# Block two's layer norms: column six closed in the last product, partial sums among its matmuls, five square buffers

## The chip, the cores and the metric

The kernel runs on one core of a Trainium2 chip. The metric is the device time of one execution in microseconds. TensorE, VectorE, ScalarE and GpSimd work side by side from instruction queues of their own and wait for each other by counters; SyncE issues most of the loads.

## The reference

Two transformer blocks stand one behind the other on x (1 x 512 tokens x 1024), float32, two layers each. The change touches only the second. Each of its layers is

```python
def _layer_norm(x, g, b):
    xf = x.astype(jnp.float32)
    mu = xf.mean(-1, keepdims=True)
    var = jnp.square(xf - mu).mean(-1, keepdims=True)
    return ((xf - mu) * lax.rsqrt(var + LN_EPS)).astype(x.dtype) * g + b

    h = x * (1.0 + sc1) + sh1
    y = _token_mixer(h, ...)
    x = _layer_norm(ALPHA * x + g1 * y, ln1_g[l], ln1_b[l])
    h = x * (1.0 + sc2) + sh2
    y = _conv_ffn(h, ...)
    x = _layer_norm(ALPHA * x + g2 * y, ln2_g[l], ln2_b[l])
```

so there are four of these norms in an execution: one (layer 0, "mix"), two (layer 0, "ffn"), three (layer 1, "mix") and four (layer 1, "ffn", whose result is the output).

## The kernel before, in words

**Layout.** X lies in SBUF transposed: eight chunks ("columns", 0 to 7) of 128 channels x 512 tokens. A mean over the channels is a sum over the eight chunks and over the partitions; the latter is a matmul with a 128 x 128 matrix of ones.

**Products.** Weights come in panels of 1 MB (raw, three slots, SyncE). Each is split for exactness into a high part (ScalarE, `split_hi`, line 754, two slots) and a low part (VectorE, `split_lo`, line 760, in the raw panel's place). The operand is split likewise (Hhi/Hlo, Mhi/Mlo, Uhi/Ulo). A chunk of a product is three matmuls, lines 782, 783 and 789. A panel gives two output columns, each summed over nk chunks (8; 6 in the last part of the FFN's down product). Where `k_outer` is set, the first panel behind a norm runs over the chunks outside, so that it can begin with the first normed chunk.

**Order.** One Python list of items (`Schedule`) is walked by every engine, and each takes from it what is its own, in that order. `product` puts the high and low split of the next panel behind a quarter of a panel's steps. All waits are on counters of the instruction that made the datum.

**The end of a branch.** `out_stages` and the last part of `ffn_stages` have four panels (p = 0 to 3), two columns each. `evict` of a column on VectorE is, from line 2081: a residual scaling (2092 or 2095; in the FFN it was done with the first part), for columns 4 to 7 a shift by -2/D times the sum of the first four columns (line 2106), and the addition of the gated product from PSUM (line 2111). That half mean mh is made behind half of panel 2: GpSimd adds columns 0 to 3 into sx (line 1698), TensorE sums it (line 2275). Columns 0 to 3 get their shift afterwards (line 2117).

**Squares and sums.** Each shifted column is squared on ScalarE (line 1837; two buffers) and added on GpSimd into qa (line 1708), in the order 0, 1, 4, 2, 3, 5, 6; xa (line 1714) adds columns 4, 5 and 6, which stand in for all because the shift made the first four's part known. Column 7 and its square are not added.

**`lnend`.** After the four panels TensorE sums, in this order, xa and qa (lines 2283, 2284), X seven (2286, same bank as xa) and square seven (2289, same bank as qa). ScalarE makes the squared mean (1842) and the mean msb (1843); VectorE the variance (2125) and X zero minus mean (2129); ScalarE the root (1845, behind a load of its table); VectorE the reciprocal (2131). GpSimd subtracts the mean from columns 1 to 7 (1720).

**`lnx`, `lnlo`.** Per column VectorE multiplies by the reciprocal (2138), ScalarE makes the high half and the full value of the next operand (1851, 1854) or the output (1857), VectorE the low half (2142). The next item is the first product, and a quarter into it the split of the second panel.

In the "mix" norm of layer 0, GpSimd issues two loads of tables (lines 1684, 1685) between its last xa and its subtractions.

Of the kernel before, what the change touches and what calls it, by code (L numbers as in the profile page):

```python
# [16 lines left out]
P = 128  # L17
# [13 lines left out]
FFN_PARTS = ((0, 8), (8, 8), (16, 6))  # L31
A_HEADS = 8
# [70 lines left out]
class Schedule:  # L103
# [19 lines left out]
    def split_ahead(self, n):  # L123
        while self.splits < min(n + 1, len(self.planned)):
            self.add("split", self.splits, self.planned[self.splits][1])
            self.splits += 1
# [15 lines left out]
    def product(self, n, nk, width, cols, rhs, k_outer=False, midway=None):  # L142

        self.begin(n)
        for _, job in cols:
            self.wide.take(job)
        self.last_use[n] = cols[-1][1]
        if k_outer:
            steps = [(k, cc, job) for k in range(nk) for cc, job in cols]
        else:  # L150
            steps = [(k, cc, job) for cc, job in cols for k in range(nk)]
        quarter, half = len(steps) // 4, len(steps) // 2
        self.add("mm", n, width, steps[:quarter], nk, rhs)
        self.split_ahead(n + 1)
        self.add("mm", n, width, steps[quarter:half], nk, rhs)
        if midway:
            midway()
        self.add("mm", n, width, steps[half:], nk, rhs)
# [287 lines left out]
def out_stages(s, n, l, column, between=lambda: None, halfway=None):  # L446

    for p in range(4):
        s.product(n, 8, 256, [(j, ("out", l, 2 * p + j)) for j in range(2)], ("M", l), k_outer=(p == 0),
                  midway=halfway if p == 2 else None)  # L450
        n += 1
        between()
        for c in (2 * p, 2 * p + 1):
            s.add("evout", l, c)
            column(c)
# [3 lines left out]
def ffn_stages(s, n, l, column, between=lambda: None, root=None, halfway=None):  # L459

    for part, (u0, nu) in enumerate(FFN_PARTS):
# [22 lines left out]
        last = part == len(FFN_PARTS) - 1  # L484
        for p in range(4):
            s.product(n, nu, 256, [(j, ("down", l, part, 2 * p + j)) for j in range(2)], ("U", l, part),
                      k_outer=(p == 0), midway=halfway if last and p == 2 else None)
            n += 1
            between()
            for c in (2 * p, 2 * p + 1):  # L490
                s.add("evdown", l, part, c)
                if last and column:
                    column(c)
    return n


def schedule_two():
# [6 lines left out]
    for l in range(DEPTH):  # L504
# [111 lines left out]
        n = out_stages(s, n, l, lambda c: ln_column(s, l, "mix", c), halfway=lambda: ln_half(s, l, "mix"))  # L616
        if l + 1 < DEPTH:
            s.add("tables", l + 1)
        layer_norm_stages(s, l, "mix", (l, "ffn"))
        n = ffn_stages(s, n, l, lambda c: ln_column(s, l, "ffn", c), halfway=lambda: ln_half(s, l, "ffn"))  # L620
        layer_norm_stages(s, l, "ffn", (l + 1, "mix") if l + 1 < DEPTH else None)
    return s

# [7 lines left out]
SQUARED = (0, 1, 4, 2, 3, 5, 6)  # L631


def ln_column(s, l, w, c):
# [3 lines left out]
    for i in {4: (0, 1, 4), 5: (2, 3, 5), 6: (6,), 7: (7,)}.get(c, ()):  # L638
        if i > 0:
            s.temp("sq", 2, ("sq", l, w, i))  # L640
        s.add("lnsq", l, w, i)


def layer_norm_stages(s, l, w, after):

    s.small.take(("mn", l, w))
    s.small.take(("ss", l, w))
    s.temp("rs", 2, ("rs", l, w))
    s.add("lnend", l, w)
    for k in range(DC):  # L650
# [5 lines left out]
    if after:  # L656
        s.add("lnlo", *after, DC - 1)

# [273 lines left out]
def block_one(nc, io, known, banks=None):  # L932
    from contextlib import ExitStack
    s = schedule_one()
    with ExitStack() as ctx:
# [174 lines left out]
        def _(act):  # L1110
# [8 lines left out]
            for kind, *a in s.items:  # L1119
                if kind == "sines":  # L1120
                    build_tables(nc, None, act, steps, "tab1", None, None, [t[:] for t in tab_tmp], cos[:], sin[:], None)
                elif kind == "split":
# [110 lines left out]
        def _(dve):  # L1233
            dve.wait_ge(gain_landed, 16)
            for kind, *a in s.items:
# [7 lines left out]
                elif kind == "split":  # L1243
# [310 lines left out]
def block_two(nc, io, known):  # L1554
    from contextlib import ExitStack
    s = schedule_two()
    with ExitStack() as ctx:
        def sem(name):
# [12 lines left out]
        coef = mem.put("coef", [P, 3, 4, 8])  # L1571
        ulow = mem.at
# [36 lines left out]
        msb = mem.again(ulo_at + 8 * SEQ * 4, area).put("msb", [P, SEQ])  # L1609
# [12 lines left out]
                    fa=fa, silu=silu, fw=fw, fv=fv)  # L1622
# [35 lines left out]
        def at_col(j):  # L1658
            return (0, 512, 896, 1152)[j]

# [16 lines left out]
        def _(pool):  # L1677
            for kind, *a in s.items:
# [21 lines left out]
                elif kind == "lnsq" and a[2] not in (0, 7):  # L1700
                    l, w, c = a
                    i = SQUARED.index(c)
                    pool.wait_ge(*after("sq", l, w, c))
                    if i == 1:
                        pool.wait_ge(*after("sq", l, w, 0))
                    else:
                        pool.wait_ge(*after("qa", l, w, SQUARED[i - 1]))
                    ng.tensor_tensor(qa[:], qa[:], k.sq[slot("sq", ("sq", l, w, c))][:], ALU.add)\  # L1708
                        .then_inc(*mark("pool", ("qa", l, w, c), ("free", ("sq", l, w, c))))
                    if c >= 5:  # L1710

                        if c == 6:
                            pool.wait_ge(*after("xa", l, w, 5))
                        ng.tensor_tensor(xa[:], X[:, 4] if c == 5 else xa[:], X[:, c], ALU.add)\
                            .then_inc(*mark("pool", ("xa", l, w, c)))
# [35 lines left out]
        def _(act):  # L1751
# [6 lines left out]
            for kind, *a in s.items:  # L1758
                if kind == "split":
# [71 lines left out]
                elif kind == "lnsq":  # L1831
                    l, w, c = a
                    dst = qa[:] if c == 0 else buf(("sq", l, w, c))
                    if c > 0:
                        reuse(act, ("sq", l, w, c))
                    act.wait_ge(*after("xc", l, w, c))
                    act_e.activation(dst, X[:, c], ACT.Square).then_inc(*mark("act", ("sq", l, w, c)))
# [39 lines left out]
        def _(dve):  # L1877
# [19 lines left out]
            for kind, *a in s.items:  # L1897
                if kind == "split":
# [182 lines left out]
                elif kind == "evout" or kind == "evdown":  # L2081
# [7 lines left out]
                    if part == 0:  # L2089
                        ready = ("scaled", l, w, c)  # L2090
                        if l == 0 and w == "mix":
                            nv.tensor_scalar(X[:, c], X[:, c], ALPHA, None, ALU.mult).then_inc(*mark("dve", ready))
                        else:
                            by = (l, "mix") if w == "ffn" else (l - 1, "ffn")
                            nv.tensor_scalar(X[:, c], X[:, c], normed(*by, 2, c), normed(*by, 3, c), ALU.mult, ALU.add)\
                                .then_inc(*mark("dve", ready))
# [348 lines left out]
```

## Time and profile before

| | |
|---|---|
| median of 3 runs | 3611.62 us (3606.71 to 3614.3) |
| the profiled execution | 3609.19 us, span 3607.4 us |
| mean granted clock of TensorE | 0.973 |
| busy: TensorE, VectorE, ScalarE, GpSimd | 93%, 59%, 36%, 18% |
| block two's four norms, end of the product before | 2178.7, 2563.3, 3199.3, 3582.3 us |

Times in rows are in us from the start of the span. A timeline row is: start, length, engine, line, operation, written tile <- read tiles, shape, count of like ones in a row; in brackets the idle time of the engine before it and what ended it. A 512-wide float32 matmul with ones shows as two records (x2). Tiles of one name are told apart by their lines. PE is TensorE, DVE VectorE, ACT ScalarE, POOL GpSimd.

### The profile page before, as it was taken

To read this page: it belongs to the slowest core of one execution; us is meant where nothing else is said; L and a number is where in the kernel's file an instruction comes from. 1 tells how busy PE (TensorE), PEld (TensorE's weight loads), DVE (VectorE), ACT (ScalarE), POOL (GpSimd) and SP (SyncE) were. 2 spreads that over 40 slices of the span, in tenths; PEclk is the share of its full clock that TensorE was granted. 3 is DMA by queue.
4 is the path that set the end of the run, shared out by engine and by line. 5 is a ranking of instruction groups with operands and counts; after the bars stand their busy time and mean duration, and the time that the engine had idled before them with its cause. 6 is when DMAs were issued, how large, how long until landed. Compare 5 with 4: busy or idle time off the path is not lost. (4 is left out here: it accounts for less than half of the span.)

```text
span 3607.4 us, 38854 instructions
## 1 busy us (share of the span) xinstructions
PE 3369.9 (93%) x15280; PEld 2678.6 (74%) x15280; DVE 2142.4 (59%) x2729; ACT 1283.3 (36%) x1648; POOL 634.0 (18%) x507
## 2 busy tenths in 40 slices
PE   7899999999999999959988998999899979989997
PEld 5677788876677788847776886888677768868886
DVE  7853666448744765437986336554568864365545
ACT  4664322235653322223223324243432232243333
POOL 1122222121212311210001123010300002131003
PEclk9999999999999999979999999999999989999998
DMA  3122445321224453221211222222211112322221
GB/s 121 44 67 82 181 187 196 108 94 54 54 75 155 179 194 143 70 91 70 70 53 53 88 99 83 94 101 92 76 66 64 65 47 70 105 70 100 94 94 70
DMA packets 72181, 344.44 MB, mean 95 GB/s; under 512 B 25152, under 2 KB 26048, under 8 KB 35648
## 3 DMA queue, kind: packets, MB, share of 16 engines
q1 hardware_dynamic: 70560, 340.17, 27.0%
q8 instruction: 122, 2.00, 0.2%
q0 software_dynamic: 432, 1.28, 0.2%
q10 hardware_dynamic: 1008, 0.51, 0.0%
q14 instruction: 59, 0.48, 0.0%
HBM read 340.51 MB, written 2.10 MB: 95 GB/s over the span
## 5 line engine op out<-in xcount | busy, mean ns | idle before, releaser
L782 PE MATMUL bank_b<-Hhi_b,whi_b 128*128 128x512 f32 x2976 | 1228.3, 413 | 106.0 <-DVE wlo_b L760 52.2
L783 PE MATMUL bank_b<-Hhi_b,wlo_b 128*128 128x512 f32 x2976 | 1176.0, 395 | 0.0
L789 PE MATMUL bank_b<-Hlo_b,whi_b 128*128 128x512 f32 x2976 | 1165.3, 395 | 0.8 <-DVE Hlo_b L2142 0.8
L760 DVE TENSOR_TENSOR wlo_b<-raw_b,whi_b 128x2048 fp32r<-128x2048 f32 (+2 forms) x290 | 625.4, 2157 | 572.4 <-ACT whi_b L754 572.2
L782 PEld LDWEIGHTS bank_b<-Hhi_b,whi_b 128*128 128x128 f32 x2976 | 570.5, 192 | 257.8 <-issue 80.3
L783 PEld LDWEIGHTS bank_b<-Hhi_b,wlo_b 128*128 128x128 f32 x2976 | 570.1, 192 | 125.8 <-issue 14.3
L789 PEld LDWEIGHTS bank_b<-Hlo_b,whi_b 128*128 128x128 f32 x2976 | 567.6, 191 | 126.1 <-DVE Hlo_b L2142 3.0
L754 ACT ACTIVATE whi_b<-raw_b 128x2048 fp32r<-128x2048 f32 (+2 forms) x290 | 511.4, 1764 | 370.6 <-PE bank_b L789 370.5
L782 PE MATMUL bank_b<-Uhi_b,whi_b 128*128 128x512 f32 x1024 | 407.5, 398 | 0.0
L783 PE MATMUL bank_b<-Uhi_b,wlo_b 128*128 128x512 f32 x1024 | 401.4, 392 | 0.0
L789 PE MATMUL bank_b<-Ulo_b,whi_b 128*128 128x512 f32 x1024 | 387.8, 392 | 0.0
L871 POOL TENSOR_TENSOR Ulo_b<-fv_b,Uhi_b 128x512 fp32r<-128x512 f32 x88 | 114.0, 1296 | 712.3 <-ACT Uhi_b L868 712.3
L782 PEld LDWEIGHTS bank_b<-Uhi_b,whi_b 128*128 128x128 f32 x1024 | 192.2, 188 | 47.2 <-issue 4.6
L783 PEld LDWEIGHTS bank_b<-Uhi_b,wlo_b 128*128 128x128 f32 x1024 | 192.2, 188 | 43.7 <-issue 1.9
L789 PEld LDWEIGHTS bank_b<-Ulo_b,whi_b 128*128 128x128 f32 x1024 | 192.1, 188 | 43.6
L1948 DVE SCALAR_TENSOR_TENSOR acc_b<-Up_b,vec_b,acc_b 128x512 f32<-128x512 f32 x240 | 192.2, 801 | 4.7
L1083 POOL TENSOR_TENSOR silu_b<-silu_b,RX_b 128x512 f32<-128x512 f32 x44 | 100.6, 2289 | 405.5 <-DVE silu_b L1447 405.5
L868 ACT ACTIVATE Uhi_b<-fv_b 128x512 fp32r<-128x512 f32 x88 | 55.6, 633 | 288.0 <-DVE fv_b L1454 168.8
L1099 POOL TENSOR_SCALAR sc_b<-sc_b,rec_b 128x256 f32<-128x256 f32 (+1 forms) x128 | 87.1, 693 | 371.6 <-DVE rec_b L1392 371.6
L857 POOL TENSOR_TENSOR ym_b<-ym_b,mt_b 128x512 f32<-128x512 f32 x48 | 67.7, 1414 | 383.6 <-DVE mt_b L849 383.6
L1417 DVE CUSTOM_DVE_ANT_0 ada_b<-ada_b,cond_b,bada_b 128x1024 f32<-128x1024 f32 x96 | 134.6, 1439 | 0.0
L871 POOL TENSOR_TENSOR Ulo_b<-ON_b,Uhi_b 128x512 fp32r<-128x512 f32 x16 | 22.3, 1396 | 602.8 <-ACT Uhi_b L868 602.8
(244 smaller groups left out, 3493.8 us busy)
## 6 DMA issues: line engine op xcount, KB each, us to landing
raw_b<-in_w SPq DMA_DIRECT2D x234, 1024.0 KB, 4.9
ada_b<-in_wada SPq DMA_DIRECT2D x48, 1024.0 KB, 7.0
raw_b<-in_w SPq DMA_DIRECT2D x40, 512.0 KB, 3.6
raw_b<-in_w SPq DMA_DIRECT2D x16, 768.0 KB, 4.3
rel_b<-in_rel SPq DMA_DIRECT2D x128, 24.0 KB, 2.4
X_keep<-in_x SPq DMA_DIRECT2D x4, 512.0 KB, 8.6
out<-X_keep SPq DMA_DIRECT2D x8, 256.0 KB, 2.1
cond_b<-in_c SPq DMA_DIRECT2D x2, 512.0 KB, 4.4
```

The lines of the kernel that those rows point to most:

```text
L754: self.nc.scalar.activation(self.whi[n % HI_SLOTS][:, 0:words], self.raw[n % RAW_SLOTS][:, 0:words], ACT.Copy).then_inc(*self.steps.mark(" ...
L760: self.nc.vector.tensor_tensor(self.wlo[n % RAW_SLOTS][:, 0:words], self.raw[n % RAW_SLOTS][:, 0:words], self.whi[n % HI_SLOTS][:, 0:words ...
L782: self.nc.tensor.matmul(out, whi[:, k, cols], xhi, start=(k == 0), stop=False)
L783: self.nc.tensor.matmul(out, wlo[:, k, cols], xhi, start=False, stop=False)
L789: mm = self.nc.tensor.matmul(out, whi[:, k, cols], xlo, start=False, stop=(k == nk - 1))
L857: nc.gpsimd.tensor_tensor(y, y, k.mt[k.slot("mt", mt)][:], ALU.add)\
L868: nc.scalar.activation(hi, src, ACT.Copy).then_inc(*steps.mark("act", ("hi",) + name))
L871: nc.gpsimd.tensor_tensor(lo, src, hi.bitcast(F32), ALU.subtract)\
L1083: nc.gpsimd.tensor_tensor(g, g, RX[:], ALU.mult).then_inc(*mark("pool", ("silu", l, c)))
L1099: nc.gpsimd.tensor_scalar(p, p, rec[:, i % 2, j:j + 1], 1.0, ALU.mult, ALU.mult)\
L1417: nc.vector.tensor_tensor_reduce(w, w, cond[:], 1.0, bada[:, l, j:j + 1], ALU.mult, ALU.add, keep.mod[:, l, j:j + 1]).then_inc(*mark("dve" ...
L1948: nv.scalar_tensor_tensor(out=acc[:, c], in0=src, scalar=w, in1=acc[:, c], op0=ALU.mult, op1=ALU.add).then_inc(*mark("dve", ("cv", l, c, t ...
```

## The change

1. `product` takes a table of hooks (step to action) and a switch for the split ahead. In the last panel of `out_stages` and `ffn_stages` there is no split at the quarter.
2. For p = 1 to 3 the eviction of the first column of a panel stands in the list at the half of the panel, not behind it.
3. Column six: its residual scaling and shift, and those of column seven, are items of their own behind column five (`lnshift`). Its eviction stands behind half of the last panel.
4. `lngather` on TensorE, before that eviction: sum of xa (now columns 4 and 5 alone) and sum of qa (without six). `lnsix`, half a column and a step later: sums of X six and of square six. Behind the product only the sums of X seven and square seven are left.
5. On GpSimd xa is one addition, before the last of qa's five.
6. Five buffers for squares (`lsq`): the old two and three more in the area of the mean.
7. ScalarE does a root of one element behind square six (`idle_root`), so that its table is loaded there; behind it stand both splits of the first panel after the norm.
8. The high split of the second panel (`round`) stands behind `lnend`, the low one (`rest`) behind the last `lnlo`.
9. GpSimd subtracts the mean from columns 1 to 6, VectorE from column 7, just before its multiplication.
10. The table loads of layer 1 stand behind the norm.

```diff
-    def product(self, n, nk, width, cols, rhs, k_outer=False, midway=None):
+    def product(self, n, nk, width, cols, rhs, k_outer=False, hooks=None, ahead=True):
...
+        hooks = dict(hooks or {})
+        if ahead:
+            hooks[len(steps) // 4] = lambda: self.split_ahead(n + 1)
+        at = 0
+        for stop in sorted(hooks):
+            self.add("mm", n, width, steps[at:stop], nk, rhs)
+            hooks[stop]()
+            at = stop
+        self.add("mm", n, width, steps[at:], nk, rhs)
...
+def closing_hooks(s, l, w, nk, p, middle):
+
+    if p == 0:
+        return {}
+    if p < 3:
+        return {nk: middle}
+
+    def gathered():
+        s.small.take(("mn", l, w))
+        s.small.take(("ss", l, w))
+        s.add("lngather", l, w)
+        middle()
+
+    return {nk: gathered, nk + nk // 2 + 1: lambda: s.add("lnsix", l, w)}
...
     for i in {4: (0, 1, 4), 5: (2, 3, 5), 6: (6,), 7: (7,)}.get(c, ()):
         if i > 0:
-            s.temp("sq", 2, ("sq", l, w, i))
+            s.temp("lsq", 5, ("lsq", l, w, i))
         s.add("lnsq", l, w, i)
+    if c == 5:
+        s.add("lnshift", l, w, 6)
+        s.add("lnshift", l, w, 7)
+    if c == 6:
+        s.split_ahead(n)
...
     s.add("lnend", l, w)
+    if after:
+        s.round_next()
     for k in range(DC):
...
     if after:
         s.add("lnlo", *after, DC - 1)
+        s.rest_next()
...
+                    if c == 5:
+                        ng.tensor_tensor(xa[:], X[:, 4], X[:, 5], ALU.add).then_inc(*mark("pool", ("xa", l, w)))
+                    ng.tensor_tensor(qa[:], qa[:], buf(("lsq", l, w, c)), ALU.add)\
+                        .then_inc(*mark("pool", ("qa", l, w, c), ("free", ("lsq", l, w, c))))
...
-                    for c in range(1, DC):
+                    for c in range(1, DC - 1):
                         ng.tensor_tensor(X[:, c], X[:, c], msb[:], ALU.subtract).then_inc(*mark("pool", ("xm", l, w, c)))
...
+                    if c == 6:
+
+                        i = 2 * l + (w == "ffn")
+                        act_e.activation(idle_root[:, i:i + 1], keep.eps[EPS2][:, 0:1], ACT.Sqrt)\
+                            .then_inc(*mark("act", ("root table", l, w)))
...
+                elif kind == "lnshift":
+                    l, w, c = a
+                    ready = ("xp", l, 1, c)
+                    if w == "mix":
+                        ready = ("scaled", l, w, c)
+                        residual(l, w, c)
+                    shift_column(dve, ready, l, w, c)
...
+                    if c == DC - 1:
+                        nv.tensor_tensor(X[:, c], X[:, c], msb[:], ALU.subtract).then_inc(*mark("dve", ("xm", l, w, c)))
...
-                elif kind == "lnend":
+                elif kind == "lngather":
                     l, w = a
                     mn, ss = ("mn", l, w), ("ss", l, w)
                     reuse(pe, mn)
                     reuse(pe, ss)
-                    pe.wait_ge(*after("xa", l, w, 6))
+                    pe.wait_ge(*after("xa", l, w))
                     nt.matmul(k.out_of(mn)[:], keep.ones[:], xa[:], start=True, stop=False, skip_group_check=True)
+                    pe.wait_ge(*after("qa", l, w, 5))
                     nt.matmul(k.out_of(ss)[:], keep.ones[:], qa[:], start=True, stop=False, skip_group_check=True)
+                elif kind == "lnsix":
+                    l, w = a
+                    pe.wait_ge(*after("xc", l, w, 6))
+                    nt.matmul(k.out_of(("mn", l, w))[:], keep.ones[:], X[:, 6], start=False, stop=False,
+                              skip_group_check=True)
+                    pe.wait_ge(*after("lsq", l, w, 6))
+                    nt.matmul(k.out_of(("ss", l, w))[:], keep.ones[:], buf(("lsq", l, w, 6)), start=False, stop=False,
+                              skip_group_check=True).then_inc(*mark("pe", ("free", ("lsq", l, w, 6))))
```

## Rows read from the trace of the kernel before

**Rows 1.** The page's first part: busy us, share of the span.

```profile
PE 3369.9 (93%) x15280; PEld 2678.6 (74%) x15280; DVE 2142.4 (59%) x2729; ACT 1283.3 (36%) x1648; POOL 634.0 (18%) x507
```

**Rows 2.** Timeline of TensorE around the four norms, behind its waits.

```profile
2182.53 1.69 PE L2283 MATMUL bank_b<-xa_b,ones_keep 128*128 128x512 f32 x2 [3.84 <-POOL xa_b L1714]
...
2212.32 0.47 PE L782 MATMUL bank_b<-Hhi_b,whi_b 128*128 128x512 f32 x1 [2.66 <-issue]
...
2568.58 2.03 PE L2283 MATMUL bank_b<-xa_b,ones_keep 128*128 128x512 f32 x2 [5.33 <-POOL xa_b L1714]
...
3232.98 0.47 PE L782 MATMUL bank_b<-Hhi_b,whi_b 128*128 128x512 f32 x1 [1.13 <-ACT fa_b L1865]
...
3584.57 1.10 PE L2283 MATMUL bank_b<-xa_b,ones_keep 128*128 128x512 f32 x2 [2.25 <-POOL xa_b L1714]
```

**Rows 3.** Timeline of TensorE, the half mean's sum inside a product.

```profile
2160.93 1.02 PE L2275 MATMUL bank_b<-sx_b,ones_keep 128*128 128x512 f32 x2
2161.39 0.80 PE L782 MATMUL bank_b<-Mhi_b,whi_b 128*128 128x512 f32 x1
```

**Rows 4.** Timeline of GpSimd in norms one and four.

```profile
2169.80 4.18 POOL L1708 TENSOR_TENSOR qa_b<-qa_b,sq_b 128x512 f32<-128x512 f32 x3 [1.51 <-ACT sq_b L1837]
2173.93 3.37 POOL L1714 TENSOR_TENSOR xa_b<-X_keep 128x512 f32<-128x512 f32 x1
...
2188.24 9.96 POOL L1720 TENSOR_TENSOR X_keep<-X_keep,msb_b 128x512 f32<-128x512 f32 x7 [4.79 <-ACT msb_b L1843]
...
3573.64 7.07 POOL L1708 TENSOR_TENSOR qa_b<-qa_b,sq_b 128x512 f32<-128x512 f32 x5 [6.29 <-ACT sq_b L1837]
...
3583.17 1.26 POOL L1714 TENSOR_TENSOR xa_b<-xa_b,X_keep 128x512 f32<-128x512 f32 x1
```

**Rows 5.** Timeline of VectorE in norms one, two and four.

```profile
2164.66 0.42 DVE L2092 TENSOR_SCALAR X_keep<-X_keep 128x512 f32<-128x512 f32 x1
...
2167.64 0.75 DVE L2111 SCALAR_TENSOR_TENSOR X_keep<-bank_b,mod_keep,X_keep 128x512 f32<-128x512 f32 x1 [1.84 <-PE bank_b L789]
...
2188.03 0.69 DVE L2125 SCALAR_TENSOR_TENSOR rs_b<-bank_b,m_b 128x512 f32<-128x512 f32 x1 [7.09 <-PE bank_b L2289]
...
2190.22 3.35 DVE L2131 RECIPROCAL rs_b<-rs_b 128x512 f32<-128x512 f32 x1 [0.18 <-ACT rs_b L1845]
...
2196.97 1.77 DVE L2142 TENSOR_TENSOR Hlo_b<-hf_b,Hhi_b 128x512 fp32r<-128x512 f32 x1
...
2208.12 0.69 DVE L2142 TENSOR_TENSOR Hlo_b<-hf_b,Hhi_b 128x512 fp32r<-128x512 f32 x1 [0.72 <-ACT hf_b L1854]
2209.93 2.29 DVE L760 TENSOR_TENSOR wlo_b<-raw_b,whi_b 128x2048 fp32r<-128x2048 f32 x1 [1.11 <-ACT whi_b L754]
...
2576.27 3.35 DVE L2131 RECIPROCAL rs_b<-rs_b 128x512 f32<-128x512 f32 x1 [0.18 <-ACT rs_b L1845]
...
3574.28 0.75 DVE L2111 SCALAR_TENSOR_TENSOR X_keep<-bank_b,mod_keep,X_keep 128x512 f32<-128x512 f32 x1 [0.85 <-PE bank_b L789]
...
3578.36 0.75 DVE L2111 SCALAR_TENSOR_TENSOR X_keep<-bank_b,mod_keep,X_keep 128x512 f32<-128x512 f32 x1 [1.53 <-PE bank_b L789]
...
3592.05 3.35 DVE L2131 RECIPROCAL rs_b<-rs_b 128x512 f32<-128x512 f32 x1 [0.18 <-ACT rs_b L1845]
```

**Rows 6.** Timeline of ScalarE, norm one: the load before the root.

```profile
2188.18 1.28 ACT L1845 ACT_TABLE_LOAD   x1
```

**Rows 7.** Windows of TensorE: stretch, busy (count), granted clock, DMA share, GB/s.

```profile
2212.00:2218.00 6.00, 5.68 (x18) 0.72 0.29 122
3214.00:3224.00 10.00, 6.58 (x15) 0.50 0.00 0
3232.00:3240.00 8.00, 7.02 (x31) 1.00 0.38 131
```

**Rows 8.** Timeline of ScalarE in block one: roots, then a square.

```profile
80.89 0.63 ACT L1179 ACTIVATE qa_b<-qa_b 128x512 f32<-128x512 f32 x1
81.43 0.58 ACT L1164 ACTIVATE sq_b<-bank_b 128x512 f32<-128x512 f32 x1
```

More of the change, by code:

```diff
@@ L484, in ffn_stages, with evict @@
         last = part == len(FFN_PARTS) - 1
+        split = last and halfway
         for p in range(4):
[L486 to L490, printed above, removed]
+            def evict(c):
                 s.add("evdown", l, part, c)
@@ L493, in ffn_stages, with middle @@
                     column(c)
+            def middle():
+                if p == 2:
+                    halfway()
+                evict(2 * p)
+            s.product(n, nu, 256, [(j, ("down", l, part, 2 * p + j)) for j in range(2)], ("U", l, part),
+                      k_outer=(p == 0), hooks=closing_hooks(s, l, "ffn", nu, p, middle) if split else None,
+                      ahead=not split or p < 3)
+            n += 1
+            between()
+            if not split or p == 0:
+                evict(2 * p)
+            evict(2 * p + 1)
     return n
@@ L1571, in block_two @@
         coef = mem.put("coef", [P, 3, 4, 8])
+        idle_root = mem.put("idle_root", [P, 4])
         ulow = mem.at
@@ L1608, in block_two @@
         qa, xa, sx, m2 = (lnb.put(n, [P, SEQ]) for n in ("qa", "xa", "sx", "m2"))
-        msb = mem.again(ulo_at + 8 * SEQ * 4, area).put("msb", [P, SEQ])
+        lnb = mem.again(ulo_at + 8 * SEQ * 4, area)
+        msb, *more_sq = (lnb.put(n, [P, SEQ]) for n in ("msb", "sq2", "sq3", "sq4"))
         mm_ = mem.again(past_tables, end)
@@ L1659, in at_col, with residual, shift_column @@
             return (0, 512, 896, 1152)[j]
+        def residual(l, w, c):
+            if l == 0 and w == "mix":
+                nv.tensor_scalar(X[:, c], X[:, c], ALPHA, None, ALU.mult).then_inc(*mark("dve", ("scaled", l, w, c)))
+            else:
+                by = (l, "mix") if w == "ffn" else (l - 1, "ffn")
+                nv.tensor_scalar(X[:, c], X[:, c], normed(*by, 2, c), normed(*by, 3, c), ALU.mult, ALU.add)\
+                    .then_inc(*mark("dve", ("scaled", l, w, c)))
+        def shift_column(dve, ready, l, w, c):
+            dve.wait_ge(*after(*ready))
+            dve.wait_ge(*after("mh", l, w))
+            names = [("free", ("mh", l, w))] if c == DC - 1 else []
+            nv.scalar_tensor_tensor(out=X[:, c], in0=k.out_of(("mh", l, w))[:], scalar=-2.0 / D, in1=X[:, c],
+                                    op0=ALU.mult, op1=ALU.add).then_inc(*mark("dve", ("xs", l, w, c), *names))
         block = ctx.enter_context(nc.Block())
@@ L2088, in _ @@
                     ready = ("xp", l, part - 1, c)
-                    if part == 0:
+                    if part == 0 and c < 6 or part == 0 and w == "ffn":
                         ready = ("scaled", l, w, c)
[L2091 to L2096, printed above, removed]
-                    name, names = ("xp", l, part, c), []
+                        residual(l, w, c)
+                    name = ("xp", l, part, c)
                     if last and c < 4:
```

94 lines of the change are left out of this document (46 added, 48 removed).

## The prediction

> **What bounds the kernel now.** I read the page's shares first, then the longest idle times of TensorE, then VectorE, ScalarE and GpSimd around the four norms of block two. The reader should see in [rows 1] that TensorE is busy for 93% of the span: only what lies in its idle time can be won, apart from its clock. Around a norm it is idle three times, and two of them have rows here [rows 2]. It ends the last product (2178.69, which is 2182.53 less 3.84 of waiting), waits for GpSimd's xa, does the four sums, waits for the first normed chunk, and waits 2.66 us more at the second panel (2212.32). The xa waits are 3.84, 5.33 and 2.25 us in norms one, two and four; norm three repeats norm one. After the sums VectorE and ScalarE are a chain: variance, root, reciprocal (3.35 us), eight chunks.
>
> **The sums inside the product.** A 512-wide sum put between product matmuls at the full clock is seen once per norm already, the half mean. Without it the next matmul would have started at 2160.93 and ended 0.40 later; it ended at 2161.39 + 0.80 [rows 3]. So one costs 0.86 us. Four of them now stand in or behind the sums' place: xa and qa in the middle, X six and its square later, 4 x 0.86 = 3.44 us longer product. X seven and its square stay behind it.
>
> **The wait that moves in with them.** The gathering stands after half of the last product, and TensorE takes its queue in order, so all remaining matmuls stand behind it. Is xa ready there? It is queued on GpSimd behind the adds of one, four, two and three; five of them take 7.07 us in a row, 1.41 each [rows 4]. *FFN norms:* the adds begin at 3573.64, xa at 3573.64 + 4 x 1.41 = 3579.28, takes 1.26 as the add of 3583.17 did, and the hand-over to TensorE costs 0.14 (3584.43 to 3584.57 [rows 2, 4]): 3580.7. Column six is done 4.08 us after column five: their evictions start at 3574.28 and 3578.36 [rows 5], so TensorE is there at 3578.2. It waits 2.5 us; qa then is ready 0.4 us later than its turn: 2.9 us. Norm two has the same code and shapes up to there, and I take the same. *Mix norms:* the product runs from about 2167.5 (column five's eviction starts at 2167.64, 0.11 behind it) to 2178.69, so its half ends at 2173.1 [rows 2, 5]. The three adds began at 2169.80; after two of them xa would start at 2172.6, end at 2173.9, and be seen at 2174.05. There I add 0.4 us for the port, below. Waits: 1.35 and 0.4, about 1.8 us.
>
> The port: xa took 3.37 us beside VectorE's weight split, where such an add takes 1.26 alone [rows 4], so GpSimd waits out a VectorE instruction, and a residual scaling of 0.42 us (the tensor_scalar of line 2092, [rows 5]) now stands twice between these adds. Bounds: 0 if both fall in GpSimd's own pauses, 0.84 if both hit; the first falls at about 2169.6, before the adds begin, so I take 0.4. The Trainium skill (SBUF — State Buffer, "SBUF: two separate sides") says that the port pair shared by VectorE and GpSimd is locked exclusively for a whole instruction, the loser fully blocked; by that both scalings count, and the two mix norms together would win 0.9 us less. The trace agrees for the weight split.
>
> The first shifts themselves are off the path: they leave VectorE's queue before column six arrives. The root table (1.28 us), the tiny root and the split of the first panel (some 2 us on ScalarE, 2.29 us on VectorE [rows 5, 6]) now run between the evictions of six and seven, after 2174; they end some 7 us later, at about 2181, before the product's end at 2183.8. If that cover went, eviction seven would stand behind the split on VectorE. The five square buffers end ScalarE's waits on GpSimd, which set nothing: the adds follow each other without a pause already.
>
> **From the product's end to the reciprocal.** After: 0.11 to the eviction of seven, 0.75 for it, 0.10 to the matmul; the square's sum ends 0.86 + 1.02 later; variance starts 0.14 on. Before, variance to reciprocal was 2188.03 to 2190.22, with the table load beside the variance and the subtraction of chunk zero beside the root: VectorE waited only 0.18 for the root [rows 5, 6]. So the missing load wins 0.14 and not 1.28; 2.05 remain. Together 5.03 us. Before it was 2190.22 - 2178.69 = 11.53 in norm one, 2576.27 - 2563.25 = 13.02 in two, and 3592.05 - 3582.33 = 9.72 in four [rows 2, 5]. So the reciprocal moves by
> - norm one: 3.44 + 1.8 + 5.03 - 11.53 = -1.26 us; norm three stands alike [rows 2];
> - norm two: 3.44 + 2.9 + 5.03 - 13.02 = -1.65 us;
> - norm four: 3.44 + 2.9 + 5.03 - 9.72 = +1.65 us. Its product had no panel split beside it, so xa came soon, and the wait now taken early costs more than it saves.
>
> **Behind the reciprocal.** GpSimd does six subtractions, not seven (9.96/7 = 1.42 each [rows 4]), and so is done when VectorE comes to the first low half, which took 1.77 us instead of 0.69 [rows 5]: 1.0 to 1.1 us won; I take 1.0 in norms one to three. VectorE's own subtraction of chunk seven (0.68, and 0.04 of hand-over) stands before the last multiplication, on the path: -0.72. The high half of the second panel no longer waits for the last chunk on ScalarE. The split on VectorE at 2209.93 had waited 1.11 for it behind the last low half [rows 5]: that is won. Balance 1.4 us in each of norms one to three. In norm three TensorE itself was late (half clock until 3224 [rows 7]) and can give back only some: 1.1, an estimate between its two ends 0 and 1.4. In norm four I take 0.3 (less contention against one more instruction). The table DMAs moved behind the subtractions on GpSimd meet nobody: their reader is hundreds of us away.
>
> Sum: -(1.26 + 1.4) - (1.65 + 1.4) - (1.26 + 1.1) + (1.65 - 0.3) = -6.7 us.
>
> **Clock.** After the 2.66 us wait at the second panel the granted clock was 0.72 of full over 6 us, part of it at half (1.2 GHz for 2.4) [rows 2, 7], which costs 6 x 0.28 = 1.7 us of TensorE; behind a wait of 1.13 us at the same place in norm three it stayed at 1.00 [rows 2, 7]. With a wait of about 1.5 left there, norm one wins 1.7. The waits of 2.5 + 0.4 us inside the two FFN products are as long as those behind which it fell: I charge 1.7 each. Net +1.7. Total -5.0 us. The profiled execution took 3609.19 us (span 3607.4); the median is 3611.62, 2.4 above. The forecast against the median is 3606.6. A measurement of this kernel can tell about 0.2%, 7.2 us.
>
> **The rivals.**
> - *The clock holds inside the FFN products* (both stall halves fall so that it isn't lowered). For it: rows show only that 1.13 us is harmless and 2.66 not, and 2.5 lies between. Then -8.4: 3603.2.
> - *TensorE restarts late everywhere*, as in norm three: at half clock it needs longer for the first panel than the splits do, and the 1.4 us behind the reciprocal are hidden anyway. Then -1.26 - 1.65 - 1.26 + 1.65 + 1.7 = -0.8: 3610.8. Against it: in norms one and two TensorE waited for the split.
> - *Slower: TensorE's wait at the gathering drags the clock down.* GpSimd's chain is the new bound of the last product, the clock falls in all four, for twice as long, 3.4 us of cost each (norm three's restart had 10 us at half [rows 7]). Then -6.7 + 13.6 = +6.9: 3618.5. It decides from 1.7 us of surcharge per norm. For it: the wait is sure in the FFN norms. Against: in the mix norms it is 1.3 and 0.4.
> - *The change doesn't do what it says: the root table isn't kept.* If the square of column seven needed another table, two loads would be paid again, about 2.0 us per norm: +3.0: 3614.6. Against it: in block one squares follow roots directly, with no load between [rows 8]. The Trainium skill (ScalarE: Activation LUTs, "Table sets: the hidden batching unit") names copy and identity as present in every set, and not Square among them.
>
> **How the numbers follow.** Forecast 0.47, clock holds 0.25, late restart 0.15, slower 0.08, table 0.05. Faster by over 0.2% (below 3604.4): most of the second case and a quarter of the first, 0.33. Slower by over 0.2%: 0.06, from the drag. Within: 0.61. The range runs from the clock case with the port bound at zero and a little less waiting (3600.5) to the late restart and the table case's lower part (3612).
>
> **What would show it.** In the changed trace: two sums in the middle of the last product with a wait for GpSimd before them (1.4 us mix, 2.5 us FFN) and two without any wait; no table load behind the variance; product end to reciprocal near 5.0 us; the low half of chunk zero near 0.7 us; a wait at the second panel of 1.5 us or less; the last norm ending later. The prediction is wrong if the sums in the middle find xa ready (then about -18 us: 9.4 of waits and 3.4 of clock less), or if the sum of chunk seven waits for VectorE.

## The result, and the profile after

| | before | after |
|---|---|---|
| median of 20 runs each | 3609.34 us (3601.22 to 3614.3) | 3614.52 us (3609.47 to 3620.33) |
| ratio after to before | | 1.0018, interval 1.0011 to 1.0025 |
| span of the profiled execution | 3607.4 us | 3611.0 us |
| mean granted clock | 0.973 | 0.976 |

The change costs 6.5 us (0.0018 x 3609; 4.0 to 9.0 by the interval). The forecast was 5.0 us less, and its range ended at 3612: the time fell outside it, on the other side of no change. What the prediction followed is nearly all there in the trace. First the timeline of TensorE, norm one (columns as in the rows above: start, length, engine, line, operation, and in brackets the idle time before it and what ended it):

```profile
2169.27 1.02 PE L2349 MATMUL bank_b<-sx_b,ones_keep 128*128 128x512 f32 x2
...
2181.14 0.40 PE L844 MATMUL bank_b<-Mlo_b,whi_b 128*128 128x512 f32 x1
2182.47 1.10 PE L2357 MATMUL bank_b<-xa_b,ones_keep 128*128 128x512 f32 x2 [0.94 <-DVE X_keep L2176]
2183.61 1.12 PE L2359 MATMUL bank_b<-qa_b,ones_keep 128*128 128x512 f32 x2
...
2184.80 0.39 PE L838 MATMUL bank_b<-Mhi_b,wlo_b 128*128 128x512 f32 x1
...
2192.98 1.12 PE L2372 MATMUL bank_b<-X_keep,ones_keep 128*128 128x512 f32 x2 [0.92 <-DVE X_keep L2176]
...
2217.70 0.47 PE L837 MATMUL bank_b<-Hhi_b,whi_b 128*128 128x512 f32 x1 [1.51 <-ACT fa_b L1940]
```

The wait of 3.84 us at xa [rows 2] has become 0.94 us within the product (the row names VectorE; xa itself ended on GpSimd at 2182.32), the wait at the second panel 1.51 instead of 2.66. The reader can check the price of the new block: L838 would have followed L844 at 2181.14 + 0.47 = 2181.61 and came at 2184.80, 3.19 us later, where two sums at 0.86 and waits of 1.8 were forecast, 3.52. The same sum in norm three gives 3.59, in norm four 4.59 (forecast 4.62). In norm two it is 5.77. There the clock fell. TensorE and its windows (stretch, busy, granted clock, DMA share, GB/s) in norm two and, last row, behind the second panel of norm one:

```profile
2568.74 2.05 PE L2357 MATMUL bank_b<-xa_b,ones_keep 128*128 128x512 f32 x2 [2.35 <-POOL xa_b L1783]
```

```profile
2568.00:2570.00 2.00, 1.25 (x2) 0.58 0.00 0
2570.00:2572.00 2.00, 2.00 (x4) 0.57 0.00 0
...
2217.70:2223.70 6.00, 6.00 (x26) 1.00 0.41 157
```

Norm four has the same wait to the hundredth, and kept its clock. Timeline of TensorE there:

```profile
3583.27 1.10 PE L2357 MATMUL bank_b<-xa_b,ones_keep 128*128 128x512 f32 x2 [2.35 <-POOL xa_b L1783]
```

VectorE in norm one, which answers to [rows 5]: the second residual scaling, which stood beside an add of GpSimd, the reciprocal, the first two multiplications and the first low half.

```profile
2178.96 0.80 DVE L1721 TENSOR_SCALAR X_keep<-X_keep 128x512 f32<-128x512 f32 x1
...
2197.04 3.34 DVE L2203 RECIPROCAL rs_b<-rs_b 128x512 f32<-128x512 f32 x1
2200.42 2.49 DVE L2212 TENSOR_TENSOR X_keep<-X_keep,rs_b 128x512 f32<-128x512 f32 x2
2202.83 1.77 DVE L2216 TENSOR_TENSOR Hlo_b<-hf_b,Hhi_b 128x512 fp32r<-128x512 f32 x1
```

The same two multiplications in the kernel before:

```profile
2193.61 3.44 DVE L2138 TENSOR_TENSOR X_keep<-X_keep,rs_b 128x512 f32<-128x512 f32 x2
```

GpSimd's adds beside that scaling:

```profile
2178.12 2.79 POOL L1784 TENSOR_TENSOR qa_b<-qa_b,sq_b 128x512 f32<-128x512 f32 x2 [1.56 <-ACT sq_b L1907]
```

ScalarE in norm one: the table is loaded where the change wants it, and the square of column seven, the copies and the root follow with no other load.

```profile
2183.15 1.28 ACT L1911 ACT_TABLE_LOAD   x1
2184.44 0.20 ACT L1911 ACTIVATE idle_root_b<-eps_keep 128x1 f32<-128x1 f32 x1
...
2193.02 0.63 ACT L1907 ACTIVATE sq_b<-X_keep 128x512 f32<-128x512 f32 x1 [6.57 <-DVE X_keep L2176]
...
2195.84 0.72 ACT L1920 ACTIVATE rs_b<-rs_b,eps_keep 128x512 f32<-128x512 f32 x1 [0.61 <-DVE rs_b L2197]
```

**The norms' account.** Two starts that every version has are taken as marks: the half mean's sum (2169.27 above, 2160.93 in [rows 3]), the reciprocal (2197.04; 2190.22), and at the end the first matmul of the second panel (2217.70; 2212.32), in norm four the end of the span. Distances in us:

| | norm one | two | three | four | sum |
|---|---|---|---|---|---|
| before | 51.39 | 48.43 | 51.39 | 38.38 | |
| after | 48.43 | 46.77 | 48.80 | 39.49 | |
| difference | -2.96 | -1.66 | -2.59 | +1.11 | -6.1 |
| forecast, without the clock | -2.66 | -3.05 | -2.36 | +1.35 | -6.7 |

So the norms won what they were to win, and the kernel is slower. The loss lies elsewhere. It is in the part of the page that the prediction never opened, the costliest groups (line, engine, operation, tiles, shapes, count | busy us, mean ns of one | idle before). Before:

```profile
L782 PE MATMUL bank_b<-Uhi_b,whi_b 128*128 128x512 f32 x1024 | 407.5, 398 | 0.0
L783 PE MATMUL bank_b<-Uhi_b,wlo_b 128*128 128x512 f32 x1024 | 401.4, 392 | 0.0
L789 PE MATMUL bank_b<-Ulo_b,whi_b 128*128 128x512 f32 x1024 | 387.8, 392 | 0.0
```

After, the same three lines:

```profile
L837 PE MATMUL bank_b<-Uhi_b,whi_b 128*128 128x512 f32 x1024 | 412.2, 403 | 0.0
L838 PE MATMUL bank_b<-Uhi_b,wlo_b 128*128 128x512 f32 x1024 | 404.6, 395 | 0.0
L844 PE MATMUL bank_b<-Ulo_b,whi_b 128*128 128x512 f32 x1024 | 391.0, 395 | 0.0
```

The same 3072 matmuls on Uhi and Ulo are busy for 1207.8 us in place of 1196.7: 11.1 us more, at a mean clock that is no lower. That sum only points the way: busy time is not spacing, and it also holds the matmuls behind the sums and those at half clock. Single chunks show it better. TensorE's timeline in the last product of norm four, one chunk's first matmul and the next chunk's, before:

```profile
3578.08 0.39 PE L782 MATMUL bank_b<-Uhi_b,whi_b 128*128 128x512 f32 x1
...
3578.76 0.39 PE L782 MATMUL bank_b<-Uhi_b,whi_b 128*128 128x512 f32 x1
```

and after:

```profile
3586.06 0.40 PE L837 MATMUL bank_b<-Uhi_b,whi_b 128*128 128x512 f32 x1
...
3586.76 0.39 PE L837 MATMUL bank_b<-Uhi_b,whi_b 128*128 128x512 f32 x1
```

A chunk takes 0.70 us where it took 0.68, with nothing between its matmuls. Block two has 544 such chunks (176 in a layer's down product and 96 in its branches, two layers): 544 x 0.02 = 10.9 us. With -6.1 from the norms that makes +4.8, against 6.5 (4.0 to 9.0) measured.

What changed for these matmuls is where their operand lies. The tiny tile of the root, `idle_root`, takes 32 bytes of a partition and was put in front of Uhi. So Uhi starts at byte 111968 in place of 111936 (added up from the allocation lines), an odd multiple of 32 where it had been a multiple of 64; every tile that block two allocates behind it moves too. That is the theory. Its rivals: that the 0.02 us belong to the changed order of work (other engines' accesses in those stretches), and that the loss is the clock's, by the new waits in the products.

### The profile page after: what moved, and what is told of

It is laid out like the page before. It is cut to its first block and busy times, and to the rows that moved or that the text cites. A ratio compares the mean times of both kernels' runs of the same rounds, so it can differ in the third digit from the quotient of the medians.

```text
span 3611.0 us, 38873 instructions
## 1 busy us (share of the span) xinstructions
PE 3384.9 (94%) x15296; PEld 2677.0 (74%) x15296; DVE 2143.1 (59%) x2733; ACT 1284.3 (36%) x1652; POOL 613.3 (17%) x495
## 3 DMA queue, kind: packets, MB, share of 16 engines
q0 software_dynamic: 432, 1.28, 0.2%
## 5 line engine op out<-in xcount | busy, mean ns | idle before, releaser
L838 PE MATMUL bank_b<-Hhi_b,wlo_b 128*128 128x512 f32 x2976 | 1174.2, 395 | 0.0
L844 PE MATMUL bank_b<-Hlo_b,whi_b 128*128 128x512 f32 x2976 | 1166.3, 395 | 0.8 <-DVE Hlo_b L2216 0.8
L838 PEld LDWEIGHTS bank_b<-Hhi_b,wlo_b 128*128 128x128 f32 x2976 | 569.3, 191 | 127.0 <-issue 14.0
L844 PEld LDWEIGHTS bank_b<-Hlo_b,whi_b 128*128 128x128 f32 x2976 | 566.3, 191 | 128.3 <-DVE Hlo_b L2216 4.5
L838 PE MATMUL bank_b<-Uhi_b,wlo_b 128*128 128x512 f32 x1024 | 404.6, 395 | 0.0
L844 PE MATMUL bank_b<-Ulo_b,whi_b 128*128 128x512 f32 x1024 | 391.0, 395 | 0.0
L838 PEld LDWEIGHTS bank_b<-Uhi_b,wlo_b 128*128 128x128 f32 x1024 | 192.1, 188 | 47.7 <-issue 2.9
L844 PEld LDWEIGHTS bank_b<-Ulo_b,whi_b 128*128 128x128 f32 x1024 | 192.0, 187 | 47.2
L2176 DVE SCALAR_TENSOR_TENSOR X_keep<-bank_b,mod_keep,X_keep 128x512 f32<-128x512 f32 x64 | 47.7, 751 | 134.5 <-PE bank_b L844 133.9
```

The costliest lines, as they stand in the source:

```text
L838: self.nc.tensor.matmul(out, wlo[:, k, cols], xhi, start=False, stop=False)
L844: mm = self.nc.tensor.matmul(out, whi[:, k, cols], xlo, start=False, stop=(k == nk - 1))
```

## The experiments

**Is it the place, and only the place?** Two edits, one that takes it out of the change and one that puts it alone into the kernel before.

```diff
 # e1_root_last, on the changed kernel
-        idle_root = mem.put("idle_root", [P, 4])
         ulow = mem.at
...
         k.rs = [mem.put(f"rs{i}", [P, SEQ]) for i in range(2)]
+        idle_root = mem.put("idle_root", [P, 4])
 # e2_pad_only, on the kernel before, block two
         coef = mem.put("coef", [P, 3, 4, 8])
+        mem.at += 32
         ulow = mem.at
```

> The change as it is, but the tile idle_root (32 bytes per partition) stands behind the last tile of block two and no longer in front of Uhi, so Uhi, Ulo and all behind them keep their addresses of before. Theory A (placement: the 1632 matmuls of block two that read Uhi or Ulo start 0.233 us apart instead of 0.227 because their operand now starts at an odd multiple of 32 bytes): 1632 x 0.0066 = 10.8 us less than the change, some 6 us less than before (ratio 0.998), U matmuls back at 0.227. Rival B (the loss lies in the norms, placement is harmless): ratio 1.002 as the change.

> The kernel before with nothing but 32 unused bytes per partition put in front of Uhi in block two. Theory A: 10.8 us slower than before, ratio 1.003, U matmuls 0.233 us apart. Rival B: ratio 1.000.

Measured: e1_root_last 3604.62 us (3596.7 to 3610.17, 11 runs), ratio to the kernel before 0.9988 (0.9979 to 0.9997); e2_pad_only 3621.41 us (3618.79 to 3623.83, 5 runs), ratio 1.0038 (1.0025 to 1.005). The median of before was 3607.21 there. The page's group of the second matmul of a chunk in e1_root_last:

```profile
L838 PE MATMUL bank_b<-Uhi_b,wlo_b 128*128 128x512 f32 x1024 | 401.9, 392 | 0.0
```

and in e2_pad_only:

```profile
L783 PE MATMUL bank_b<-Uhi_b,wlo_b 128*128 128x512 f32 x1024 | 404.7, 395 | 0.0
```

32 unused bytes, with no other edit, slow the kernel before by 13.7 us (9 to 18; 10.9 worked out) and bring 395 ns; the change without them in that place has 392 again. By the ratios, each to the kernel before as it ran beside it, it takes 10.8 us less than with them (1.0018 less 0.9988). Both rivals fall: e2_pad_only has the old order and the old waits. The change without its side effect is faster than the kernel before by 4.3 us (1 to 8), near the 5.0 forecast. Its three lines on Uhi and Ulo still add up to 1200.4 us of busy time, 3.7 above the kernel before: that part of the 11.1 us is not the place's.

The operand's own place is not the whole price. Chunks on Hhi, which lies in front of the padding and did not move, are slower too at some places in the mixers. Two chunks of TensorE's timeline, from one start to the next but one, in e2_pad_only and in the kernel before:

```profile
2026.53 0.40 PE L782 MATMUL bank_b<-Hhi_b,whi_b 128*128 128x512 f32 x1
...
2027.92 0.39 PE L782 MATMUL bank_b<-Hhi_b,whi_b 128*128 128x512 f32 x1
```

```profile
2018.70 0.39 PE L782 MATMUL bank_b<-Hhi_b,whi_b 128*128 128x512 f32 x1
...
2020.06 0.39 PE L782 MATMUL bank_b<-Hhi_b,whi_b 128*128 128x512 f32 x1
```

1.39 us in place of 1.36. Set side by side chunk by chunk, where both traces have one without a wait, the 1246 chunks on Hhi in block two take 2.0 us more in all than in the kernel before, nearly all of it in some 140 of them, and the 90 on Mhi 0.35 more; from e1_root_last to the changed kernel it is 1.9 and 0.3. With 10.9 that is some 13 us, near the 13.7 measured. So what is shown is the price of the 32 bytes. That the start of the operand sets it is the simplest reading for Uhi, whose chunks all went from 0.68 to 0.70; for Hhi it must be another tile that moved, and which one no run tells.

**What grade of alignment?** The tile made 64 bytes, so that Uhi starts at 112000, a multiple of 128.

```diff
 # e3_root_64, on the changed kernel
-        idle_root = mem.put("idle_root", [P, 4])
+        idle_root = mem.put("idle_root", [P, 16])
```

> The change with idle_root in its place but 64 bytes per partition long, so that Uhi starts at a multiple of 64 again, though 64 bytes further on than before. Theory A in the form that the start modulo 64 decides: as e1_root_last, ratio 0.998. Rival: that any move of the tiles costs (their place against the weight panels): ratio 1.002.

Measured: 3606.59 us (3601.03 to 3609.39, 11 runs), ratio 0.9995 (0.9987 to 1.0004).

```profile
L838 PE MATMUL bank_b<-Uhi_b,wlo_b 128*128 128x512 f32 x1024 | 401.5, 392 | 0.0
L844 PE MATMUL bank_b<-Ulo_b,whi_b 128*128 128x512 f32 x1024 | 389.3, 393 | 0.0
```

The chunks follow at 0.69, 0.69, 0.68 us in turn, 0.687 in the mean: a third grade, which neither expectation had. By the times alone the run can't be told from e1_root_last (0.9979 to 0.9997); the chunks tell it. Uhi at 111936 (64 past a multiple of 128) gives 0.68, at 112000 (a multiple of 128) 0.687, at 111968 0.70. Beside it this trace bears on the clock. Its wait at the gathering of norm two is longer than the changed kernel's, and the clock stayed (timeline, then window):

```profile
2564.18 1.10 PE L2357 MATMUL bank_b<-xa_b,ones_keep 128*128 128x512 f32 x2 [2.48 <-POOL xa_b L1783]
```

```profile
2566.00:2570.00 4.00, 4.00 (x17) 1.00 0.00 0
```

In e1_root_last both FFN norms wait 2.52 us and the clock falls in both (windows):

```profile
2564.00:2566.00 2.00, 2.00 (x5) 0.50 0.00 0
...
3572.00:3574.00 2.00, 2.00 (x4) 0.52 0.00 0
```

Of six such waits of 2.35 to 2.52 us in three kernels three lowered the clock and three did not. The length of the wait does not decide it.

**The gathering later.** The wait at xa is a matter of place: with both pairs of sums where the second pair stood, half a column later, xa is there before its turn comes.

```diff
 # e4_gather_late, on e1_root_last
-    def gathered():
+    def sums():
         s.small.take(("mn", l, w))
         s.small.take(("ss", l, w))
         s.add("lngather", l, w)
-        middle()
+        s.add("lnsix", l, w)
 
-    return {nk: gathered, nk + nk // 2 + 1: lambda: s.add("lnsix", l, w)}
+    return {nk: middle, nk + nk // 2 + 1: sums}
```

> As e1_root_last, and the sums of xa and qa stand at the place of those of column six, ten or thirteen steps into the last product, when GpSimd has both. Theory (TensorE's wait for xa costs what it lasts: 0.9 and 1.3 us in the mix norms, 2.35 us each in the FFN norms, and in norm two a stretch at half clock of 3.4 us behind it): 7 us or more less than e1_root_last, some 13 us less than before (ratio 0.9963), no wait for xa in the product. Rival (the wait is hidden by what comes behind): the same as e1_root_last.

Measured: 3593.03 us (3589.84 to 3596.85, 5 runs), ratio 0.9959 (0.9945 to 0.9972), 11.6 us less than e1_root_last. TensorE in norm two no longer waits for xa within the product; qa is still some 0.28 us behind its turn there (1.14 between the starts of the two sums, where 0.86 is one sum), and the wait for the eviction of column seven stays:

```profile
2558.78 0.39 PE L844 MATMUL bank_b<-Ulo_b,whi_b 128*128 128x512 f32 x1
2559.05 1.10 PE L2357 MATMUL bank_b<-xa_b,ones_keep 128*128 128x512 f32 x2
2560.19 1.12 PE L2359 MATMUL bank_b<-qa_b,ones_keep 128*128 128x512 f32 x2
...
2565.34 1.12 PE L2372 MATMUL bank_b<-X_keep,ones_keep 128*128 128x512 f32 x2 [0.93 <-DVE X_keep L2176]
```

The four distances are 46.82, 42.83, 46.83 and 36.71 us, where e1_root_last has 48.35, 47.10, 48.77 and 40.79: -1.5, -4.3, -1.9, -4.1, together -11.8. The FFN norms lose their wait and the half clock behind it, the mix norms their wait. So the waits that moved in with the sums cost about what the prediction charged (1.8 us in a mix norm, 2.9 + 1.7 in an FFN norm), and they were avoidable.

**Parts of the change, one by one, on e4_gather_late** (one run each; the distances carry the reading, not the single time).

```diff
 # e7_no_root_preload: the root of one element left out
-                    if c == 6:
-                        i = 2 * l + (w == "ffn")
-                        act_e.activation(idle_root[:, i:i + 1], keep.eps[EPS2][:, 0:1], ACT.Sqrt)\
-                            .then_inc(*mark("act", ("root table", l, w)))
 # e8_seven_on_gpsimd
-                    for c in range(1, DC - 1):
+                    for c in range(1, DC):
...
-                    if c == DC - 1:
-                        nv.tensor_tensor(X[:, c], X[:, c], msb[:], ALU.subtract).then_inc(*mark("dve", ("xm", l, w, c)))
 # e9_splits_at_quarter: the second panel's splits a quarter into the first
-    if after:
-        s.round_next()
...
-        s.rest_next()
```

> e4_gather_late without the root of one element behind square six, so that the table is loaded when the root itself comes. My step: the load hid beside the variance already and wins 0.14 us per norm: from the half mean's sum to the reciprocal 26.17, 22.18, 26.18 and 22.14 us become longer by 0 to 0.3 us each. Rival (the preload wins the load's whole 1.28 us): 1.3 us longer each.

> e4_gather_late, with chunk seven's subtraction back on GpSimd. My steps: VectorE's copy of it costs 0.72 us on the path, six instead of seven on GpSimd wins 1.0. From the reciprocal to the second panel's first matmul e4_gather_late takes 20.65 us in norm one. If only the first step holds: 19.9. If both hold: 20.9. From the reciprocal to the end of norm four (14.57 there): 14.3 if only the first, 15.3 if both.

> e4_gather_late with the second panel's splits back at the quarter of the first product. My step: 1.12 us per norm, so that the second panel starts 21.8 us behind the reciprocal instead of 20.65 in norms one to three. Rival (VectorE's end sets it anyway): 20.65.

| | sum to reciprocal (norm one) | reciprocal to second panel | norm four, reciprocal to end | time |
|---|---|---|---|---|
| e4_gather_late | 26.17 | 20.65 | 14.57 | 3593.03 |
| e7_no_root_preload | 26.43 | 20.80 | 14.47 | 3591.23 |
| e8_seven_on_gpsimd | 26.18 | 21.01 | 15.35 | 3588.90 |
| e9_splits_at_quarter | 26.18 | 21.86 | 14.56 | 3602.22 |

The table loaded beforehand is worth 0.26 us up to the reciprocal (0.14 forecast) and 0.4 in all, 0.2 in norm four; the load of 1.28 us is back in front of the root in e7_no_root_preload, but VectorE has its subtraction to do meanwhile:

```profile
2189.65 1.28 ACT L1915 ACT_TABLE_LOAD   x1
```

Column seven on VectorE is worth 0.36 us in norms one to three (1.0 less 0.72 = 0.28 forecast) and 0.8 in norm four. The wait that it removes on VectorE stands, in e8_seven_on_gpsimd, at the multiplication behind the first low half, not at the low half:

```profile
2194.93 1.77 DVE L2214 TENSOR_TENSOR Hlo_b<-hf_b,Hhi_b 128x512 fp32r<-128x512 f32 x1
2196.63 1.76 DVE L2210 TENSOR_TENSOR X_keep<-X_keep,rs_b 128x512 f32<-128x512 f32 x1
```

The place of the second panel's splits is worth 1.2 us (1.11 forecast). In e9_splits_at_quarter the split of VectorE waits again for the high half:

```profile
2217.10 2.29 DVE L812 TENSOR_TENSOR wlo_b<-raw_b,whi_b 128x2048 fp32r<-128x2048 f32 x1 [1.11 <-ACT whi_b L806]
```

That puts TensorE's wait at the second panel at 2.72 us in norms one to three, where e4_gather_late has 1.51, and behind it the clock falls to half in norms one and three (windows of norm one and norm three) and stays in norm two:

```profile
2221.00:2223.00 2.00, 2.00 (x6) 0.50 0.01 4
3228.00:3230.00 2.00, 2.00 (x6) 0.50 0.00 0
```

At 1.6 us each, as behind norm one of the kernel before, that is 3.2 us more. So the move of the splits is worth its 1.2 us and, more often than not, the clock.

The times of e8 and e7 lie below that of e4_gather_late although their distances are longer by 2.0 and 1.4 us in the four norms: single runs of these kernels lie several us apart, so no order of these versions is read from them. Of the 9.2 us that e9_splits_at_quarter took more, its distances show 3.6 and the clock 3.2; the rest is of that size.

**Does the rule hold elsewhere?** Block one has its own Uhi, at 119136, an odd multiple of 32, and 480 chunks at 0.70 us from the start. Padding moves it.

```diff
 # e5_block_one_aligned, on the kernel before, block one: Uhi at 119168, a multiple of 128
         cos, sin = mem.put("cos", [P, SEQ]), mem.put("sin", [P, SEQ])
+        mem.at += 32
         ulow = mem.at
 # e6_late_aligned: the same on e4_gather_late
 # e10_late_aligned_64_of_128, on e4_gather_late: Uhi at 119232, 64 past a multiple of 128
+        mem.at += 96
```

> The kernel before with 32 unused bytes per partition in front of Uhi in block one, where Uhi and Ulo have begun at an odd multiple of 32 bytes all along (three matmuls of a chunk take 0.70 us there, 0.68 in block two). Placement theory: the 1440 matmuls of block one that read them come down to 0.68 per three, 480 x 0.02 = 9.6 us less, ratio 0.9973. Rival (block one's 0.70 has another cause): ratio 1.000.

> e4_gather_late and the 32 bytes of e5_block_one_aligned together. If the two are independent: ratio 0.9959 x 0.9973 = 0.993, some 24 us less than before. If one takes from the other: no better than 0.996.

> As e6_late_aligned, but with 96 bytes instead of 32, so that block one's Uhi starts 64 past a multiple of 128, as every operand does whose three matmuls take 0.680 us (in e6 it starts at a multiple of 128 and they take 0.687). If the start modulo 128 decides in three grades: 480 x 0.007 = 3.3 us less than e6_late_aligned, ratio about 0.9928, block one's U chunks at 0.680. If 0.687 belongs to block one: the same as e6_late_aligned.

Measured: e5_block_one_aligned 3605.0 us (3600.43 to 3612.74, 11 runs) beside 3610.31 of before, ratio 0.9992 (0.9983 to 1.0001): the 9.6 us expected did not come, and alone it is inconclusive (its chunks went to 0.687, which is 480 x 0.013 = 6.2 us, just inside the interval). e6_late_aligned 3586.72 us (3581.53 to 3593.82, 5 runs), ratio 0.9937 (0.9923 to 0.995): the fastest of all, 22.7 us (18 to 28) below the kernel before. e10_late_aligned_64_of_128 3594.43 us (3590.57 to 3597.44, 5 runs) beside 3607.37 of before, ratio 0.9961 (0.9947 to 0.9974). Two chunks of block one's down product in e5_block_one_aligned, from one start to the same of the pair behind:

```profile
646.19 0.39 PE L782 MATMUL bank_b<-Uhi_b,whi_b 128*128 128x512 f32 x1
...
647.57 0.39 PE L782 MATMUL bank_b<-Uhi_b,whi_b 128*128 128x512 f32 x1
```

and in e10_late_aligned_64_of_128:

```profile
646.09 0.40 PE L837 MATMUL bank_b<-Uhi_b,whi_b 128*128 128x512 f32 x1
...
647.49 0.40 PE L837 MATMUL bank_b<-Uhi_b,whi_b 128*128 128x512 f32 x1
```

1.38 us for two chunks at 119168, and 1.40 at 119232, as at 119136. A multiple of 128 gives Uhi 0.69 in both blocks, and block one's Mhi, which the same padding moves from 172384 to 172416, goes from 0.70 to 0.687 as well (nine of its chunks from 384.93 to 391.11 us in e5_block_one_aligned, from 384.94 to 391.24 before). But 64 past a multiple of 128, which gives 0.68 in block two, gives 0.70 here, against what was expected of e10_late_aligned_64_of_128: the remainder of 128 alone does not set the grade.

The last run moved the operand of block two's mixer, whose chunks take 0.70 us in every version, by 1024 bytes.

```diff
 # e11_m_moved, on e4_gather_late: Mhi of block two from 182976 to 184000
-        mm_ = mem.again(past_tables, end)
+        mm_ = mem.again(past_tables + 1024, end)
```

> e4_gather_late with Mhi and Mlo of block two 1024 bytes further on (same remainder of 128). M's three matmuls take 0.70 us although it starts 64 past a multiple of 128. If higher address bits decide: 0.680 and the half mean's sum to the reciprocal 0.7 us shorter in norms one and three. If it isn't the address: unchanged.

Measured: 3591.17 us, and the group (of both blocks' mixers) is unchanged, as are the distances:

```profile
L844 PE MATMUL bank_b<-Mlo_b,whi_b 128*128 128x512 f32 x256 | 96.0, 395 | 0.0
```

Mhi was tried at 182976, 184000 and (in e3_root_64) 183040, and it stays at 0.70. What holds it there is open.

## Why the prediction was wrong

**The step that failed.** The sum has no term for `idle_root` as a tile. The prediction costs "the tiny root" as an instruction hidden on ScalarE and says nothing of the line that gives it memory; its terms stop at the norms. That line moved Uhi, Ulo and all behind them by 32 bytes and cost 10.9 us in 1632 matmuls, most of them hundreds of us away from any norm, and some 2 us more in others. e2_pad_only shows it by itself, with 13.7 us (9 to 18). None of the five cases had it. Two stood on the slower side: the clock dragged down by the gathering in all four norms (3618.5), where it fell in one, and the root table not kept, whose 3614.6 is the measured time to 0.1 us. That is chance: no table is loaded at the root in any of the four norms, and e1_root_last, with the same order of work, is faster than the kernel before.

**The steps that held.**
- *A sum costs 0.86 us in the product.* The two of column six in norm four start at 3588.16 and 3589.02, 0.86 apart.
- *The waits.* Forecast 1.4 and 2.5 at xa, measured 0.94 and 1.33 in the mix norms and 2.35 twice in the FFN norms. The wait at qa, forecast 0.4, is 0.28 (1.14 between the starts of the two sums, less 0.86). In norm one the add of xa began at 2181.05, behind two adds that took 2.79 together, no more than adds elsewhere (1.41 each [rows 4]): GpSimd lost nothing to the residual scalings. It is VectorE that paid there, 0.80 in place of 0.42 for the second, at 2178.96, while the first of these adds was under way. The Trainium skill (SBUF — State Buffer, "SBUF: two separate sides") has the shared port pair with whichever of the two starts first for its whole instruction, and the other fully blocked; this row agrees (0.80 is 0.38 more), and it is the other way round from what the prediction charged.
- *Product end to reciprocal:* the product ended at 2192.06 (2192.98 less 0.92), the reciprocal began at 2197.04: 4.98 us, forecast 5.03.
- *Norm four loses:* +1.11, forecast +1.35.
- *Behind the reciprocal:* 20.66 instead of 22.10 us, -1.44, forecast -1.4. The place was named wrong: the first low half still takes 1.77, where 0.7 was expected, and the gain is at the two multiplications before it, 2.49 for both in place of 3.44.
- *The clock.* After the shorter wait at the second panel it stays at 1.00 and 14 matmuls need 3.3 us instead of 4.9: 1.6 won, 1.7 forecast. Of the two falls charged to the FFN products one came, at 1.15 us (5.77 less 4.62) instead of 1.7.
- *The table is kept* over the square of column seven. That rival fell, and so did the late restart: all of the 1.4 us came through, in norm three too.

Norm three gave 2.59 (2.36 forecast), norm one 2.96 (2.66), norm two 1.66 with its fall of the clock inside. With the clock behind norm one the stretches that the prediction covered gained 6.1 + 1.6 = 7.7 us, against 5.0 forecast. Of the signs listed ahead of the result one failed, the low half of chunk zero near 0.7 us; the others came, but they looked only at the norms. The one view that would have shown the loss at once is the comparison of the mean durations of the large groups, in which nothing was expected.

**The balance.** -6.1 in the norms, -1.6 behind norm one, +10.9 on Uhi and Ulo, +2.3 on Hhi and Mhi: +5.5. The medians differ by 5.2, the ratio says 6.5 (4.0 to 9.0); the spans of the two traces differ by 3.6. What is left is of the size by which like stretches of code outside the norms differ between two traces, and isn't assigned.

## What to carry to other kernels

Read the allocation lines of a diff as part of the change: whatever is put in front of a large operand moves it, and a move of 32 bytes was paid here in every matmul that read it. Put small new tiles last, and compare the mean duration of the costliest groups before and after, whatever the change is about. Where sums are moved into a product, place them behind the moment at which their slowest input is there, and not at the first seam that is free.

## What the hardware showed that was not expected

- A matmul of 128 x 512 in a product starts every 0.227, 0.229 or 0.233 us (a third of 0.68, 0.687 and 0.70), at the same granted clock and with no wait, by where the tiles of the program start in a partition. With the operand at an odd multiple of 32 (Uhi at 111968 and 119136, Mhi at 172384 and 183008) it is 0.233 or a little more. At multiples of 128 it is 0.229 for Uhi at 112000 and 119168 and for block one's Mhi at 172416, but 0.233 for block two's Mhi at 183040. At 64 past a multiple of 128 it is 0.227 for Uhi at 111936, and 0.233 for Uhi at 119232 and for Mhi at 172480, 182976 and 184000. What sets the grade among these is open, as is whether Uhi, Ulo or their distance counts: they always moved together, and with all the tiles behind them.
- Some chunks slow down by 10 to 17 ns when other tiles than their operand move by 32 bytes (Hhi in block two, e2_pad_only beside the kernel before).
- Waits of the same 2.35 us, in the same code, once lowered TensorE's clock to half and once did not; of three waits of 2.72 us in e9_splits_at_quarter two did.
